# Where the steps of a recurrence and of an attention stand between the large matmuls of a projection: inverses begun earlier, attention two turns ahead, turns in pairs

## The chip, the core and the metric

The kernel runs on one core of a Trainium2 chip. The metric is the device time of one execution in microseconds (us), lower is better; the time before is the median of three runs. The engines are named as in the profile: PE is TensorE's matmul, PEld its weight load, DVE is VectorE, ACT is ScalarE, POOL is GpSimd, and SP is SyncE, which issues DMAs.

## What is computed

The reference is two programs in a row. The first (two layers of mixers, cross attention and a gated network of width 2816, 1024 columns, 512 rows) is not touched. The second is cut here to what matters:

```python
def second_block(x, c, norm_g, w_ada, b_ada, w_in, ...):
    h = rms_norm(x, norm_g) * (1.0 + scale) + shift
    proj = h @ w_in                                  # 512 x 1024 times 1024 x 4224
    ps, pa = token_shift(proj[..., :D_SHIFT], mu_shift), proj[..., D_SHIFT:]
    y_r, g_r = rwkv7_mix(ps, ...)                    # recurrence over 512 rows, 8 heads of 64
    q, ka, va, g_a = jnp.split(pa, 4, axis=-1)
    y_a = chunk_band_attention(q, ka, va, ...)       # 8 heads of 64, chunks of 64 rows
    y = jnp.concatenate([y_r * silu(g_r), y_a * silu(g_a)], axis=-1)
    return x + gate * (y @ w_out)                    # 512 x 1024 times 1024 x 1024

def rwkv7_step(state, inp):
    r_t, w_t, k_t, v_t, a_t, b_t = inp
    sa = einsum('bhij,bhj->bhi', state, a_t)
    state = state * w_t + sa * b_t + v_t * k_t
    return state, einsum('bhij,bhj->bhi', state, r_t)
```

## The kernel before

Every large product is taken in three passes (`mm3`, lines 365 to 367): operands are split into a high part XH or WH and a low part XL or WL, and three matmuls of 128x128 weights by 512 columns add up in one PSUM bank. I call these the large matmuls. ACT makes the high part of each chunk of weights (`hi_to`, L332), DVE the low part (`lo_to`, L342).

The second block is laid out in `dense_pe`, `dense_act`, `dense_dve` and `dense_pool`, one for each engine, in the same order. The projection has nine stages: k and w, and then seven, named in `BESIDE`, beside which the small work goes: r, v, aq, ak, g, av, ag. Each stage has 96 large matmuls. Between them `side()` is called: after every 12 large matmuls in r and v (8 calls each), after every 6 in the others (16 calls each). I number these calls 1 to 96 and call them places: r has 1 to 8, v 9 to 16, aq 17 to 32, ak 33 to 48, g 49 to 64, av 65 to 80, ag 81 to 96. At each place `side()` takes one turn (one `next`) of every generator that takes part in the stage. Each engine has its own copy of each generator; what one engine does in a turn and what another does in the same turn are tied by semaphores alone. All engines work their instructions off in this order, so that a wait holds all that is queued behind it.

The generators are:

- `rwkv`, the recurrence. Its turns in order: 10 of `prep`, 13 of the inverse of block 0 with `tail`, and then for t = 1, 2, 3 the 6 turns of `state(t-1)` beside the 12 of `inverse(t)` (`in_turns` takes one turn of each at a time and ends with the longest), with the 8 of `normed(t-2)`; at last `state(3)` beside `normed(2)`, and `normed(3)`. With one turn spent before place 1, `inverse(0)` stands at places 10 to 22, `inverse(1)` at 23 to 34, `inverse(2)` at 35 to 46, `inverse(3)` at 47 to 58, the state's turns at 23 to 28, 35 to 40, 47 to 52 and 59 to 64, and `normed(3)` at 67 to 74.
- An inverse (`inverse_pe`, L2530) takes a block of 128 rows through five levels. Its turn 0 makes the masked products "ba" (L2546) and its turn 1 the products "l" (L2561) and "ka" (L2546); from then on an even turn is "x" (L2575, 32 matmuls of 64x64) and an odd one "t" (L2589 and L2595, 32 each; in the last, turn 11, L2595 alone). Turn 4 adds four more products (L2609, L2616). DVE masks what comes out (L2656 to L2685), ACT copies (L2633, L2641). Turn 1 on DVE is the long one: L2668 to L2679 and two L2656.
- A state's three turns per chunk of 64 rows are "w" (L2712, added by DVE in four parts, L2764 and L2767, the last two of which empty the two banks), "u" (L2723) and "bd" with "by" (L2734, L2739).
- `norm_qk` at places 33 to 48 (behind four idle turns) and 49 to 60; its four transposes (L1889) fall on 44 to 47 and 56 to 59.
- `late`, the attention (`att_turns`, L1946): 38 turns and an end, behind four idle turns, so that its turn 1 is at place 69. An odd turn transposes the probabilities of two heads' row blocks (L1993, 2, 4, 6 or 8 transposes in all) and every fourth one first takes the product with the values (`values`, L2005); an even one makes scores (L1981) for two more, on which DVE adds the bias and takes the maximum (L2046 to L2051) and ACT the exponentials (L2017); DVE scales the probabilities of the turn before (L2060).
- `closing`, beside ag, makes the gate's row (L2878) and joins the recurrence's parts.

`key_sums_pe` (L2296) makes the sums of squares of the keys in four groups of four matmuls; the first group is taken ahead of stage r, and the other three, one each, after 3, 6 and 9 large matmuls of r (`each` in `gemm_c`).

After place 96 a loop of 11 passes (`second_pe`, `second_act`, `second_dve`) takes the rest of the attention, one turn in each pass, and beside it on PE one `out_part_pe` (6 large matmuls, a row block t and a chunk c of the first half of the last product). `out_part_pe(t, 0)` waits for `split_dve(t)`, which waits for `split_act(t)`; chunk 2 waits for the low part of its weights. Then come four parts of chunk 3 and 96 large matmuls of the second half, and DVE closes with the gate and the sum.

PSUM has 8 banks. `Banks.take` hands out the bank that has been idle longest in the order of the program, and the taker waits until the last reader of its former content has emptied it (`vacant`). While aq, ak or av runs, four banks are held by the stage, and four go round among all small work; each of the stage's is given back in its last four places (45 to 48 for ak).

## Time and profile before

| | us |
|---|---|
| median of three runs | 1762.18 (1760.67 to 1764.33) |
| the profiled execution, its own time | 1760.65 |
| its span, first to last instruction | 1758.8 |
| PE busy in it | 1728.8 |
| DVE busy | 1110.8 |
| ACT busy | 684.7 |
| POOL busy | 184.4 |

TensorE's granted clock is full (tenths 9) in all 40 slices of the page. The span is 1.85 us shorter than the execution's own time. A matmul is shown longer than it holds the engine: a large one is shown with 0.39 or 0.40 us, and the next starts 0.23 us after it, so that the busy share of PE hides short waits. What counts is the distance between starts.

### The profile page before, as it was taken

What the parts mean: (1) busy time and instruction counts of PE and PEld (TensorE: products, weight loads), DVE (VectorE), ACT (ScalarE), POOL (GpSimd) and SP (SyncE); (2) the same over time, 40 slices, a digit from 0 to 9 for tenths busy, and PEclk for the clock granted to TensorE, in tenths of its full rate; (3) what the DMA queues carried; (4) which work ended last, traced back from release to release, by engine and by line L of the source; (5) the groups of instructions that cost most, each with busy time, mean ns of one, the idle gap of its engine ahead of it and who ended that gap; (6) DMA issues with size and microseconds to landing.
All of it is one profiled execution on the core that took longest, in us unless ns stands there. A gap on an engine that the chain in (4) does not pass through costs nothing.

```text
span 1758.8 us, 27808 instructions
## 1 busy us (share of the span) xinstructions
PE 1728.8 (98%) x11461; PEld 1447.6 (82%) x11461; DVE 1110.8 (63%) x1624; ACT 684.7 (39%) x1045; POOL 184.4 (10%) x246
## 2 busy tenths in 40 slices
PE   8999999999999999999999999999998999999998
PEld 7888988988888879888998888888886767777766
DVE  5567266454568795454726755567988585566784
ACT  5332352232235643213235232223554543345452
POOL 4202001200011112000210200001112000011000
PEclk9999999999999999999999999999999999999999
DMA  9882912973345858833492265455683422112412
GB/s 301 259 217 99 252 39 79 279 230 110 126 138 186 260 166 204 247 97 118 114 283 77 83 204 156 143 183 185 201 277 108 153 65 81 34 43 62 169 37 84
DMA packets 175453, 270.44 MB, mean 154 GB/s; under 512 B 10488, under 2 KB 97780, under 8 KB 174560
## 3 DMA queue, kind: packets, MB, share of 16 engines
q1 hardware_dynamic: 147488, 189.90, 34.2%
q0 software_dynamic: 26368, 73.51, 15.7%
q10 hardware_dynamic: 1472, 5.26, 0.8%
q8 instruction: 91, 1.49, 0.4%
q14 instruction: 34, 0.28, 0.0%
HBM read 253.67 MB, written 61.09 MB: 179 GB/s over the span
## 4 chain that ended last, share of the span: by engine, by line
PE 88%; DVE 7%; issue 2%; ACT 1%; DMA 1%; POOL 1%; SPq 0%; ACTq 0%; DVEq 0%
PE ps L365 26%; PE ps L367 26%; PE ps L366 26%; DVE WL L342 2%; PE ps L1007 2%; PE ps L554 1%; PE ps L2575 1%; PE ps L2595 1%; PE ps L2589 1%; DMA RAW<-ffn_w_down 1%; PE ps L1981 0%; DVE SM L1637 0%; PE ps L2609 0%; DVE LATE L2656 0%; PE ps L2712 0%
## 5 line engine op out<-in xcount | busy, mean ns | idle before, releaser
L342 DVE TENSOR_TENSOR WL<-RAW,WH 128x1024 fp32r<-128x1024 f32 x325 | 393.3, 1222 | 387.7 <-ACT WH L332 387.2
L332 ACT ACTIVATE WH<-RAW 128x1024 fp32r<-128x1024 f32 x325 | 341.0, 1058 | 559.8 <-PE ps L367 450.6
L365 PE MATMUL ps<-XH,WH 128*128 128x512 f32 (+1 forms) x1416 | 524.6, 370 | 2.6 <-DVE WL L342 1.5
L367 PE MATMUL ps<-XH,WL 128*128 128x512 f32 (+1 forms) x1416 | 518.1, 366 | 0.0
L366 PE MATMUL ps<-XL,WH 128*128 128x512 f32 (+1 forms) x1416 | 517.9, 366 | 0.0
L365 PEld LDWEIGHTS ps<-XH,WH 128*128 128x128 f32 x1416 | 267.4, 189 | 50.1 <-issue 5.3
L367 PEld LDWEIGHTS ps<-XH,WL 128*128 128x128 f32 x1416 | 267.3, 189 | 43.3
L366 PEld LDWEIGHTS ps<-XL,WH 128*128 128x128 f32 x1416 | 267.5, 189 | 40.7
L365 PE MATMUL ps<-WH,XH 128*128 128x512 f32 x696 | 279.1, 401 | 7.9 <-DVE WL L342 7.0
L367 PE MATMUL ps<-WH,XL 128*128 128x512 f32 x696 | 271.9, 391 | 0.0
L366 PE MATMUL ps<-WL,XH 128*128 128x512 f32 x696 | 271.6, 390 | 0.0
L365 PEld LDWEIGHTS ps<-WH,XH 128*128 128x128 f32 x696 | 130.8, 188 | 39.5 <-DVE WL L342 8.0
L367 PEld LDWEIGHTS ps<-WH,XL 128*128 128x128 f32 x696 | 130.7, 188 | 27.8
L366 PEld LDWEIGHTS ps<-WL,XH 128*128 128x128 f32 x696 | 130.9, 188 | 25.4 <-issue 0.7
L721 POOL TENSOR_SCALAR SM<-SM 128x1 f32<-128x1 f32 x28 | 33.0, 1179 | 513.9 <-DVE SM L707 513.7
L1292 ACT ACTIVATE SCR<-SCR,VEC 128x512 f32<-128x512 f32 x44 | 31.8, 723 | 103.9 <-DVE SCR L1338 103.9
L561 ACT ACTIVATE XH<-ps 128x512 fp32r<-128x512 f32 x48 | 25.8, 599 | 98.6 <-PE ps L554 98.6
L1344 DVE TENSOR_TENSOR BIG<-SCR,ps 128x512 f32<-128x512 f32 x44 | 30.1, 688 | 31.6 <-ACT SCR L1292 31.6
L2633 ACT ACTIVATE SCR<-ps 128x512 f32<-128x512 f32 x32 | 17.4, 595 | 58.0 <-PE ps L2595 58.0
L365 PE MATMUL ps<-WH,MH 128*128 128x256 f32 (+1 forms) x136 | 39.5, 291 | 0.0
L366 PE MATMUL ps<-WL,MH 128*128 128x256 f32 (+1 forms) x136 | 39.4, 290 | 0.0
L367 PE MATMUL ps<-WH,ML 128*128 128x256 f32 (+1 forms) x136 | 39.4, 290 | 0.0
(404 smaller groups left out, 2063.7 us busy)
## 6 DMA issues: line engine op xcount, KB each, us to landing
RAW<-ffn_w_up SPq DMA_DIRECT2D x176, 256.0 KB, 3.5
weight_sums<-ffn_w_down POOLq DMA_DIRECT2D x12, 1536.0 KB, 18.5
RAW<-w_in SPq DMA_DIRECT2D x33, 512.0 KB, 3.9
RAW<-xa_wkv SPq DMA_DIRECT2D x32, 512.0 KB, 7.5
RAW<-weight_sums SPq DMA_DIRECT2D x32, 512.0 KB, 4.6
weight_sums<-ffn_w_down POOLq DMA_DIRECT2D x12, 1280.0 KB, 31.1
RAW<-c_w_in SPq DMA_DIRECT2D x24, 512.0 KB, 7.2
LATE<-w_ada SPq DMA_DIRECT2D x24, 512.0 KB, 5.2
```

The costliest lines, as they stand in the source:

```text
L332: e.activation(halves_of(i)[0][:, :, 0:w], raw(i)[:, :, 0:w], ACT.Copy).then_inc(*w_hi.up(i))
L342: e.tensor_tensor(wl[:, :, 0:w], raw(i)[:, :, 0:w], wh[:, :, 0:w].bitcast(F), ALU.subtract).then_inc(*w_lo.up(i))
L365: e.matmul(o, lh, rh, start=start, stop=False)
L366: e.matmul(o, lh, rl, start=False, stop=False)
L367: return e.matmul(o, ll, rh, start=False, stop=stop)
L554: r = e.transpose(b[:, 128 * k:128 * k + 128], x[:, 128 * (4 * q + k):128 * (4 * q + k) + 128], ident)
L561: e.activation(hi[:, 4 * q:4 * q + 4, 128 * t:128 * t + 128], k4(ps.tile((n, t, q))[:, :]), ACT.Copy).then_inc(*x_hi.up((n, t, q)))
L721: e.tensor_scalar(vr[:, t:t + 1], mv[:, t, 1:2], 1e-5, None, ALU.add).then_inc(*ln_g.up((n, t, "eps")))
L1007: r = e.matmul(b[:, 256 * (t % 2):256 * (t % 2) + 256], qT[:, 2 * h + k, 128 * t:128 * t + 128], KT[:, 2 * h + k, :], start=k == 0, stop=k ...
L1292: e.activation(gc[i], gc[i], ACT.Gelu_apprx_tanh, bias=vec(f"fcb{l}", j)).then_inc(*ffn_a.up(("gelu", l, j)))
L1344: e.tensor_tensor(hT[:, j, :], gc[i], ps.tile((("up", l, nb), i))[:, :], ALU.mult).then_inc(*ps.empties((("up", l, nb), i), ffn_v, ("h", l ...
L2575: r = e.matmul(bs[g][rows_of_x(lv, of[i], cp), 64 * i:64 * i + 64], BAs[t % 2][pps[cp], of[i], 0, :], Tt[pps[cp], in_t.index(of[i]), :], s ...
```

## The change

- The recurrence. The four inverses are made once and taken in parts. `inverse(1)` gives 10 of its 12 turns beside `state(0)`; its last two stand beside the first two of `inverse(2)`. The next 8 of `inverse(2)` stand beside `state(1)` and `normed(0)`, and its last two beside the first two of `inverse(3)`. The other 10 of `inverse(3)` stand beside `state(2)` and `normed(1)`. The rest is as it was.
- The attention begins behind two idle turns instead of four.
- In av and ag (`PAIRED`) nothing is done at an odd call of `side()`, and two turns of every generator at an even one.
- The loop after ag: PE takes two turns and two `out_part_pe` in each of four passes, and one last turn between the parts of chunk 2. ACT and DVE have 9 passes instead of 11, with the high and low parts of the weights moved.
- `key_sums_pe` is one piece ahead of stage r, and `each` is gone.

The diff, without the lines that only rename `four_behind(x)` to `behind(4, x)` for `norm_qk`:

```diff
-    def gemm_c(e, stage, nm, side=None, per=2, each=iter(())):
+    def gemm_c(e, stage, nm, side=None, per=2):
...
-                next(each, None)
...
+    PAIRED = ("av", "ag")
...
+        held = [0]
+
         def side():
-            for r in runs:
-                next(r, None)
+            held[0] += 1
+            turns = 1 if name not in PAIRED else 2 if held[0] % 2 == 0 else 0
+            for n in range(turns):
+                for r in runs:
+                    next(r, None)
...
-        sums = key_sums_pe(e)
-        next(sums)
+        key_sums_pe(e)
         next(run)
...
-            if t == 3:
-                r.then_inc(*pr_pe.up("kk8"))
-                ps.back("kk8")
-            yield
+        r.then_inc(*pr_pe.up("kk8"))
+        ps.back("kk8")
...
+        iv = [inverse(e, t) for t in range(4)]
         yield from prep(e)
-        yield from in_turns(inverse(e, 0), tail(e))
-        yield from in_turns(state(e, 0), inverse(e, 1))
-        yield from in_turns(state(e, 1), inverse(e, 2), normed(e, 0))
-        yield from in_turns(state(e, 2), inverse(e, 3), normed(e, 1))
+        yield from in_turns(iv[0], tail(e))
+        yield from in_turns(state(e, 0), turns_from(iv[1], 10))
+        yield from in_turns(iv[1], turns_from(iv[2], 2))
+        yield from in_turns(state(e, 1), turns_from(iv[2], 8), normed(e, 0))
+        yield from in_turns(iv[2], turns_from(iv[3], 2))
+        yield from in_turns(state(e, 2), iv[3], normed(e, 1))
         yield from in_turns(state(e, 3), normed(e, 2))
         yield from normed(e, 3)
 
-    def four_behind(run):
-        for n in range(4):
+    def turns_from(run, n):
+        for _ in range(n):
+            next(run)
+            yield
+
+    def behind(turns, run):
+        for n in range(turns):
             yield
         yield from run
...
-        late = four_behind(att_pe_run(e))
+        late = behind(2, att_pe_run(e))
...
-        for n in range(11):
+        for t in range(4):
             next(late, None)
-            if n < 8:
-                out_part_pe(e, n // 2, n % 2)
-            elif n < 10:
-                out_part_pe(e, n - 8, 2)
-        for t in (2, 3):
+            next(late, None)
+            for c in range(2):
+                out_part_pe(e, t, c)
+        for t in range(4):
+            if t == 2:
+                next(late, None)
             out_part_pe(e, t, 2)
...
     def second_act(e):
-        for n in range(11):
+        for n in range(9):
...
-            if n == 7:
+            if n == 5:
                 hi_to(e, n_out2 + 4)
...
     def second_dve(e):
-        for n in range(11):
+        for n in range(9):
...
-            if n == 8:
+            if n == 6:
                 lo_to(e, n_out2 + 4)
```

## Rows read from the trace of the kernel before

**Rows 1.** The page, part 1: busy time of each engine.

```profile
PE 1728.8 (98%) x11461; PEld 1447.6 (82%) x11461; DVE 1110.8 (63%) x1624; ACT 684.7 (39%) x1045; POOL 184.4 (10%) x246
```

**Rows 2.** Windows: stage ak, stage ag, attention's rest; columns PE, PEld, DVE, ACT, POOL.

```profile
1519.00:1573.00 54.00, 51.85 (x1080) 41.23 (x1072) 30.98 (x63) 22.83 (x44) 5.91 (x6) 1.00 0.15 42
...
1656.00:1697.00 41.00, 40.76 (x248) 29.66 (x246) 33.74 (x82) 21.16 (x58) 0.00 (x0) 1.00 0.17 51
1697.00:1725.00 28.00, 25.31 (x140) 17.40 (x139) 18.70 (x38) 14.09 (x34) 0.00 (x0) 1.00 0.18 57
```

**Rows 3.** Timeline of PE, places 29 and 30: start, length, line, operation.

```profile
1510.81 0.40 PE L367 MATMUL ps<-WH,XL 128*128 128x512 f32 x1
1511.14 0.69 PE L2575 MATMUL ps<-SCR,LATE 64*64 64x64 f32 x32
1511.76 0.50 PE L365 MATMUL ps<-WH,XH 128*128 128x512 f32 x1
1512.10 0.40 PE L366 MATMUL ps<-WL,XH 128*128 128x512 f32 x1
...
1513.03 0.39 PE L367 MATMUL ps<-WH,XL 128*128 128x512 f32 x1
...
1513.86 0.65 PE L2595 MATMUL ps<-SCR 64*64 64x64 f32 x32
1514.44 0.50 PE L365 MATMUL ps<-WH,XH 128*128 128x512 f32 x1
```

**Rows 4.** Timeline of PE at one group of the key sums.

```profile
1397.53 0.39 PE L367 MATMUL ps<-XH,WL 128*128 128x512 f32 x1
1397.76 0.95 PE L2296 MATMUL ps<-GB,LATE 128*128 128x8 f32 x8
1398.56 0.48 PE L365 MATMUL ps<-XH,WH 128*128 128x512 f32 x1
```

**Rows 5.** Timeline of PE at a turn of eight transposes, place 81.

```profile
1656.71 0.40 PE L367 MATMUL ps<-XH,WL 128*128 128x512 f32 x1
1656.95 1.03 PE L1993 MATMUL ps<-CST,GB 128*128 128x128 f32 x8
1657.74 0.48 PE L365 MATMUL ps<-XH,WH 128*128 128x512 f32 x1
```

**Rows 6.** Waits of PE from place 33 to the end: total, times, longest.

```profile
PE ps L2546 <- issue: 1.4, 2, 1.0
PE ps L365 <- DVE WL L342: 1.1, 1, 1.1
PE ps L365 <- issue: 0.9, 1, 0.9
PE ps L2589 <- DVE SCR L2685: 0.9, 2, 0.5
PE ps L1993 <- DVE GB L2060: 0.8, 2, 0.4
PE ps L2712 <- DVE GB L2775: 0.7, 1, 0.7
```

**Rows 7.** Timeline of DVE at places 35 and 36, where `inverse(2)` begins.

```profile
1527.34 0.77 DVE L2767 TENSOR_TENSOR LAST<-LAST,ps 64x256 f32<-64x256 f32 x2
...
1530.66 0.69 DVE L2668 TENSOR_TENSOR LATE<-LATE,GB 128x512 f32<-128x512 f32 x1
...
1533.88 1.28 DVE L2656 TENSOR_TENSOR LATE<-ps,GB 128x512 f32<-128x512 f32 x2
1535.08 1.22 DVE L342 TENSOR_TENSOR WL<-RAW,WH 128x1024 fp32r<-128x1024 f32 x1
```

**Rows 8.** Groups of DVE and ACT by line, 1697 to 1725: busy and mean ns.

```profile
L2051 DVE TENSOR_REDUCE SM<-GB 128x2 f32<-128x768 f32 (+1 forms) x2 | 2.2, 1086 | 0.1
L2928 DVE TENSOR_TENSOR XL<-LATE,XH 128x512 fp32r<-128x512 f32 x2 | 1.4, 692 | 1.6 <-ACT XH L2924 1.6
...
L2017 ACT ACTIVATE GB<-GB,SM 128x384 f32<-128x384 f32 (+1 forms) x4 | 2.6, 661 | 6.7 <-DVE SM L2051 6.7
```

More of the change, by code:

```diff
@@ L2140, in dense_pe @@
             else:
-                gemm_c(e, ("in2", name), 4, side, PER.get(name, 4), sums)
+                gemm_c(e, ("in2", name), 4, side, PER.get(name, 4))
     def silu_act(e, m):
@@ L2974, in second_pe @@
     def second_pe(e):
-        late = four_behind(att_pe_run(e))
-        dense_pe(e, rwkv(e, prep_pe, tail_pe, inverse_pe, state_pe, normed_pe), {"ak": four_behind(norm_qk_pe(e, 0)), "g": norm_qk_pe(e, 1)}, late, closing_pe(e))
-        for n in range(11):
+        late = behind(2, att_pe_run(e))
+        dense_pe(e, rwkv(e, prep_pe, tail_pe, inverse_pe, state_pe, normed_pe), {"ak": behind(4, norm_qk_pe(e, 0)), "g": norm_qk_pe(e, 1)}, late, closing_pe(e))
+        for t in range(4):
             next(late, None)
-            if n < 8:
-                out_part_pe(e, n // 2, n % 2)
-            elif n < 10:
-                out_part_pe(e, n - 8, 2)
-        for t in (2, 3):
+            next(late, None)
[4 more added lines that the diff above has]
+                next(late, None)
             out_part_pe(e, t, 2)
@@ L2989, in second_act @@
     def second_act(e):
-        late = four_behind(att_act_run(e))
-        dense_act(e, rwkv(e, prep_act, tail_act, inverse_act, state_act, normed_act), {"ak": four_behind(norm_qk_act(e, 0)), "g": norm_qk_act(e, 1)}, late, closing_act(e))
-        for n in range(11):
+        late = behind(2, att_act_run(e))
+        dense_act(e, rwkv(e, prep_act, tail_act, inverse_act, state_act, normed_act), {"ak": behind(4, norm_qk_act(e, 0)), "g": norm_qk_act(e, 1)}, late, closing_act(e))
+        for n in range(9):
             next(late, None)
@@ L3009, in second_dve @@
     def second_dve(e):
-        late = four_behind(att_dve_run(e))
-        dense_dve(e, rwkv(e, prep_dve, tail_dve, inverse_dve, state_dve, normed_dve), {"ak": four_behind(norm_qk_dve(e, 0)), "g": norm_qk_dve(e, 1)}, late, closing_dve(e))
-        for n in range(11):
+        late = behind(2, att_dve_run(e))
+        dense_dve(e, rwkv(e, prep_dve, tail_dve, inverse_dve, state_dve, normed_dve), {"ak": behind(4, norm_qk_dve(e, 0)), "g": norm_qk_dve(e, 1)}, late, closing_dve(e))
+        for n in range(9):
             next(late, None)
@@ L3033, in second_pool @@
         mask_pool(e)
-        dense_pool(e, rwkv(e, prep_own, tail_own, inverse_turns, state_turns, normed_pool), {"ak": four_behind(norm_qk_pool(e, 0)), "g": norm_qk_pool(e, 1)}, iter(()), iter(()))
+        dense_pool(e, rwkv(e, prep_own, tail_own, inverse_turns, state_turns, normed_pool), {"ak": behind(4, norm_qk_pool(e, 0)), "g": norm_qk_pool(e, 1)}, iter(()), iter(()))
     def out_part_pe(e, t, c):
```

## The prediction

> **What bounds the kernel now.** I read the busy times first [rows 1], then the windows by stage [rows 2], then the timeline of PE about single groups of small matmuls [rows 3 to 5], then PE's waits [rows 6], and last the queues of DVE and ACT where these waits arise [rows 7, 8]. PE is busy nearly all the time; DVE has 33.74 of 41 us in ag and 30.98 of 54 in ak, so it isn't full, and can only hold PE for short times where a turn needs it at once. The Trainium skill (Perfetto Trace Analysis, Identifying the Most-Contended Engine) warns that a matmul's busy share doesn't tell how near the peak PE is, and would go by the weight loads: here 82% against 98% [rows 1], so there is room inside a busy PE. The rows show the same: a large matmul is shown with 0.40 us though the next can start 0.23 us after it. So I count in distances between starts. The change removes no matmul. What it can save is what PE loses between kinds of work, and what it waits.
>
> **The price of a break.** At place 29, from the last large matmul before the group to the first after it are 1511.76 - 1510.81 = 0.95 us, less 0.23 for the large one itself: 0.72 for 32 small ones. At place 30 with 64 (L2589's 32 stand ahead of L2595's) it is 1.41 - 0.23 = 1.18 [rows 3]. So 32 more cost 0.46, and 0.72 - 0.46 = 0.26 is there whatever the number. The second large matmul after the group comes 0.34 after the first instead of 0.23, 0.11 more. A break for 64x64 work costs 0.37 us. Eight transposes take 1.03 - 0.23 = 0.80, which at 0.10 each leaves no fixed part [rows 5]; I give their break under 0.1. A group of key sums takes 0.80 as well, for eight records shown with 0.95 [rows 4]: again next to nothing but the loads.
>
> The Trainium skill (TensorEngine Tiling, Key Properties) says that going from one tiling mode to another drains TensorE. The rows agree: 64*64 pays 0.37, while 128*128 transposes, in the mode of the large matmuls, pay nearly nothing. It speaks against the pairs in av and ag: a pair of transposes and scores (64*128) still has both changes of mode, so nothing of that kind is saved.
>
> **Part by part.**
>
> *Key sums in one piece.* Three groups move ahead of stage r and lose their own break: 3 x 0.07 = 0.2 us (0 to 0.4). The wait for the squares stood ahead of the first group before too, and `lora` at place 1 is reached after the same work. The sums come 2 us earlier at DVE, but DVE's next step waits for `lora`, so that gives nothing.
>
> *Inverses begun earlier.* Places 10 to 64 all have 64x64 work now; after it 10 to 60. Four groups join others: 4 x 0.37 = 1.5 us. `normed(3)` ends at place 70 and not 74, beside nothing that waits for it. On SP's queue the loads that wait for the last "by" (`back_y`, `back_x`) can start four places sooner, before stage av's end, and no other DMA stands in another order.
>
> *Waits in ak and g.* These waits stand in rows 6 with 1.4, 0.9 and 0.7 (two more of 0.4 each are not shown): about 3.8 us in sum, most of it at places 36 to 38 and 48 to 50, right behind the first two turns of an inverse. That is where the change acts, for turn 1 is the long one on DVE: from L2668 to the end of the second L2656 4.5 us, and where `lo_to` comes behind it 1.2 more [rows 7]. After the change this turn stands at places 34 and 44, in one group with the last turn of the inverse ahead. There, with four banks in turn, "t" takes two, "l" two, and "ka" has to take those of "t" again: PE waits for ACT's two copies, about 0.5 us, as "ka" waited for the copies of "u" before (0.5 and 1.0).
> At place 34 the rest is lighter than it was at 36: no adds of the state stand ahead of it in DVE's queue, and `lo_to` comes two places later, at 36. I get 0.6 us for "x" at place 35, so 1.1 against 1.8 by the distances between starts.
> At place 44 it is heavier. `lo_to` stands at 44 itself, `norm_qk` holds one of the four banks from 44 on, and at 45 only three are free when the state's "w" takes two and "x" two: the second of "x" is that of the first "w". It is emptied by the third of DVE's four adds [two of them in rows 7, 0.77], behind 4.5 + 1.2. Counted from the start of PE's group at 44: DVE begins at 1.0, is through with "ka" at 5.7, with `lo_to` at 6.9, with the add at 8.1; PE has finished "w" at 6.0. So 2.1 us, with 0.4 for the bank of "w" and 0.5 for "ka" 3.0 us, against 2.5 now. Together 4.1 for 4.3: I take a gain of 0.2, between a loss of 3 (both queues one `lo_to` and the adds longer) and a gain of 2.
>
> *Attention in pairs.* Some 13 groups of transposes join the scores behind them, at 0.04 each 0.5 us (0 to 1.2). Between scores and their transposes stood 5 x 6 = 30 large matmuls, now 3 x 12 = 36, and between the scaling on DVE and the transposes 24 instead of 18, so DVE and ACT have more time, not less. The waits of DVE for PE come in fewer and longer pieces; it has 7 us to spare in the 41 of ag [rows 2].
>
> *The end of the attention.* From 1697 to 1725 PE has 28.00 - 25.31 = 2.7 us idle [rows 2], in four waits: 0.9 for the first split ahead of `out_part_pe(0, 0)`, 0.8 in two for scaled probabilities, 1.1 for the low part of chunk 2 [rows 6]. Each hides 0.17 more, for the matmul ahead of it is shown 0.17 longer than it holds the engine: 3.5 us. After the change two groups more (values and scores, over 4 us) stand ahead of `out_part_pe(0, 0)`, which covers the split; the waits for probabilities get 12 large matmuls (2.8 us) a step instead of 6; chunk 2 is wanted after 48 large matmuls behind the last scores, not after 30. Those three go. Two come. The values of the third pair stand two turns behind the copies of their last transposes with no large matmul between: 0.4 us. And on ACT `split_act(2)` now stands behind the last exponentials, which wait for DVE's maximum [rows 8]: my queue, from the last matmul of ag, is scores at 2.1, their maximum 4.4, two exponentials 5.7, tanh 6.2, three DVE operations of 0.69 8.2, the last scores (four operations of 0.42 to 0.48) and maximum 11.0, exponentials 12.4, the split on ACT 13.0 and on DVE 13.7. PE wants it at 12.7: 1.0 us. So 3.5 - 1.4 = 2.1 (from 0, where DVE arrives 2 us later, to 3.5).
>
> **The sum.** 0.2 + 1.5 + 0.2 + 0.5 + 2.1 = 4.5 us. Against the profiled execution: 1760.65 (span 1758.8 and 1.85 around it) becomes 1756.15. The median of the runs shown is 1.5 above that execution, so 1757.7.
>
> **Rivals.**
> 1. *The waits at the joined turns take it back.* For it: the three free banks at 45 and the queue of DVE. Against it: before 44 DVE has idle time. With the loss of 3 instead of the gain of 0.2 the sum is 1.3: 1761.
> 2. *Slower.* Both meetings of two inverses make PE wait for the whole of DVE's queue, 4.5 + 1.2 + 1.5 = 7.2 us each, as it would if "ka" and "x" got their banks only after DVE is empty. That is 14.4 for 4.3, less the 4.3 of the other parts: 5.8 slower, 1768. It decides from 8 us lost over the sum, 4 per meeting. Against it: PE's own work between covers 4 us of each queue, and at 34 no `lo_to` is in it.
> 3. *Every joined group saves a full break.* If the break weren't tied to the kind of matmul, the 13 pairs would give 13 x 0.37 = 4.8 instead of 0.5: 1753.4. Rows 5 speak against it. By the rule of the Trainium skill on drains (TensorEngine Tiling, Key Properties) it would not happen.
> 4. *The end is covered wholly* (DVE meets the last split in time) and the meeting at 34 costs nothing: 1.4 + 1.1 more, 1755.2.
> 5. *It doesn't do what it says:* DVE or ACT holds the new order back so that the four places saved turn up as waits of the state's chain ("w", "u", "bd") in g. Then only the end's 2 us are left: 1760. I count it with the first.
>
> **How the numbers follow.** Forecast 0.58, with its own range 1755.5 to 1760; rivals 1 and 5 0.22; rival 2 0.07; rival 3 0.04; rival 4 0.09. A measurement of this kernel tells 0.2% from no change, 3.5 us, which is 1758.7. Over two thirds of the forecast's range and rivals 3 and 4 lie below it: faster 0.55; rivals 1 and 5 and the rest: same 0.38; slower 0.07. The range takes in rival 4, nearly all of rival 3 and rival 1 with the runs' own spread of 2 us: 1753 to 1763.
>
> **What would show it.** Right: PE has no wait over 0.3 from place 62 to 96; the place at which "x" follows "w" (L2575 after L2712) with a wait of about 2 us once, for DVE L2767; `out_part_pe(0, 0)` without a wait; a wait of about 1 us for XL (L2919) in the third pass; from the first L2546 of the recurrence to its last "by" four places of six large matmuls less. A pair in ag should take as long as its two places, less 0.1. Wrong: waits over 3 us at the joined turns, or an ACT or DVE queue that puts the splits later than 15 us after ag.

## The result and the profile after

The changed kernel takes 1768.87 us (median of 8 runs, 1763.98 to 1771.27), the kernel before 1762.66 beside it; the ratio is 1.0031, 95% interval 1.0022 to 1.0041. It is slower, by about 6 us or 0.3%, and lies outside the range that was forecast. With all later runs of the kernel before, its median is 1762.2, against which the experiments are read.

The profiled execution has a span of 1767.3 us. Part 1 of its page answers to [rows 1]: DVE, ACT and POOL work within 2 us of what they did, PE is shown 5.0 us longer, with the same number of matmuls.

```profile
PE 1733.8 (98%) x11461; PEld 1453.4 (82%) x11461; DVE 1111.9 (63%) x1624; ACT 685.5 (39%) x1045; POOL 186.4 (11%) x246
```

More PE time for the same matmuls is a matter of the clock, or of matmuls that are stretched. So I laid the large matmuls of the two traces side by side: their order is the same in both, and the time from the start of one to the start of a later one tells where time went. The times in the first column are those of the kernel before.

| Stretch of the kernel before | before | after | difference |
|---|---|---|---|
| 10.7 to 1329.6, untouched | 1318.88 | 1318.96 | +0.1 |
| 1329.6 to 1388.0, untouched | 58.40 | 60.89 | +2.5 |
| 1388.0 to 1427.9, key sums | 39.84 | 43.07 | +3.2 |
| 1427.9 to 1468.6, before the states | 40.79 | 40.76 | 0.0 |
| 1468.6 to 1727.5, recurrence and attention | 258.84 | 261.71 | +2.9 |
| 1727.5 to 1754.5, last output chunks | 26.97 | 26.97 | 0.0 |

The first stretch, which no kernel here changes, takes between 1318.8 and 1325.6 us in the profiles of the kernels below. So where single profiles are compared, it is stretch by stretch and not by their totals.

**The key sums.** The program's 16 narrow matmuls stand in the profile as 32 records of 8 columns; they are counted as records here. The windows of PE of the changed kernel (columns: window, length, PE busy, granted clock, DMA share, GB/s) show a granted clock of 0.50, that is its 1.2 GHz level, from within the group of sums on (half from 1401.2, for 6.8 us):

```profile
1398.00:1402.50 4.50, 4.50 (x35) 0.86 0.40 117
1402.50:1407.50 5.00, 5.00 (x14) 0.50 0.01 3
1407.50:1412.00 4.50, 4.50 (x18) 0.94 0.00 0
```

In the profile of the kernel before no window of this stretch is under 1.00; two of them, with the five engines' busy times ahead of the clock:

```profile
1398.00:1402.00 4.00, 4.00 (x30) 3.75 (x30) 0.09 (x1) 1.85 (x2) 0.00 (x0) 1.00 0.42 123
1402.00:1406.00 4.00, 4.00 (x18) 2.12 (x17) 0.64 (x3) 2.43 (x4) 0.00 (x0) 1.00 0.00 0
```

The timeline of PE (start, length, line, operation) has the group itself, the counterpart of [rows 4], and the large matmuls behind it, whose starts are 0.43 us apart and not 0.23:

```profile
1398.58 4.42 PE L2300 MATMUL ps<-GB,LATE 128*128 128x8 f32 x32
1402.85 0.77 PE L365 MATMUL ps<-XH,WH 128*128 128x512 f32 x1
1403.42 0.63 PE L366 MATMUL ps<-XL,WH 128*128 128x512 f32 x1
1403.85 0.63 PE L367 MATMUL ps<-XH,WL 128*128 128x512 f32 x1
```

PE waits for nothing here and is shown busy 4.50 of 4.50 us; when the clock fell it had done matmuls of 8 columns and nothing else for 2.6 us, since 1398.58. The Trainium skill (TensorE: Matmul & The Clock Gate, Part 1: The HAM clock gate) ties this clock to how busy the engine has been, and gives 0.427 us from start to start for 512 columns at the low level. The rows agree with that distance (0.43), and they show that work can be dense in the timeline and the clock fall all the same.

The 2.5 us of the untouched stretch are a fall too (granted clock 0.5 from 1346.6 to 1353.4). A second profile of the changed kernel (f3 below) has none there, and those of a1, a2, a3, b1 and others have one. So it comes and goes between executions of one program; whether the change makes it more frequent is not shown.

**The recurrence and the attention.** PE's waits from place 33 to the end (total, times, longest) answer to [rows 6]. The changed kernel's lines stand a few lower or higher: its L2548, L2577, L2591, L2597 and L2687 are L2546, L2575, L2589, L2595 and L2685 of before. In the same way the first values are L2004 or L2005, the gates L2880 or L2884, the diagonals L2901 or L2905, the keys' squares L1904 or L1905 and their sums L1915 or L1916.

```profile
PE ps L2577 <- issue: 3.5, 2, 1.8
PE ps L2597 <- DVE SCR L2687: 1.7, 1, 1.7
PE ps L2004 <- ACT VL L2197: 1.3, 1, 1.3
PE ps L2880 <- DVE SCR L2901: 1.2, 1, 1.2
PE ps L365 <- DVE XL L2921: 0.8, 1, 0.8
PE ps L2548 <- ACT LATE L2635: 0.8, 2, 0.4
```

Of [rows 6] the wait for L342, that for the first split and those for L2060 are gone, as forecast. In their place stand four that were not in the sum: 1.75 of the first row (place 43), L2597 (place 54), L2004 (the turn of place 81, now taken at 82) and L2880 (83, now at 84). The rest of the first row is place 45, 1.73, which was forecast with 2.1.

### The profile page after: what moved, and what is told of

Read it like the earlier page. It is cut to its first block, busy times and chain, and to the rows that moved or that the text cites. A ratio compares the mean times of both kernels' runs of the same rounds, so it can differ in the third digit from the quotient of the medians.

```text
span 1767.3 us, 27808 instructions
## 1 busy us (share of the span) xinstructions
PE 1733.8 (98%) x11461; PEld 1453.4 (82%) x11461; DVE 1111.9 (63%) x1624; ACT 685.5 (39%) x1045; POOL 186.4 (11%) x246
## 3 DMA queue, kind: packets, MB, share of 16 engines
q8 instruction: 91, 1.49, 0.3%
## 4 chain that ended last, share of the span: by engine, by line
PE 89%; DVE 7%; issue 2%; DMA 1%; ACT 1%; POOL 1%; SPq 0%; ACTq 0%; DVEq 0%
PE ps L365 26%; PE ps L367 26%; PE ps L366 26%; DVE WL L342 2%; PE ps L1006 2%; PE ps L553 1%; PE ps L2577 1%; PE ps L2597 1%; DMA RAW<-ffn_w_down 1%; PE ps L2591 1%; PE ps L2004 1%; PE ps L1980 0%; PE ps L2611 0%; PE ps L2736 0%; DVE SM L1636 0%
## 5 line engine op out<-in xcount | busy, mean ns | idle before, releaser
L342 DVE TENSOR_TENSOR WL<-RAW,WH 128x1024 fp32r<-128x1024 f32 x325 | 393.4, 1222 | 389.8 <-ACT WH L332 389.4
L715 DVE SCALAR_TENSOR_TENSOR XR<-XR,SM,GB 128x1024 f32<-128x1024 f32 x24 | 30.8, 1283 | 12.5 <-POOL SM L722 12.5
```

Of the source, the lines that this page charges most:

```text
L342: e.tensor_tensor(wl[:, :, 0:w], raw(i)[:, :, 0:w], wh[:, :, 0:w].bitcast(F), ALU.subtract).then_inc(*w_lo.up(i))
L715: e.scalar_tensor_tensor(out=x, in0=x, scalar=rs[:, t:t + 1], in1=b, op0=ALU.mult, op1=ALU.add).then_inc(*ln_v.up((n, t)))
```

## The experiments

Each kernel is built from the kernel before or from the changed one. The diffs are shortened; a comment says what isn't shown. "+3.8" means against the 1762.2 of the kernel before; "clock" is the mean granted clock of all runs of a kernel. That of the kernel before is 0.9992, that of the changed kernel 0.9965; 0.001 of a span is 1.8 us. A run's clock is given to 0.001, and it varies from run to run, so that the mean of a kernel is uncertain by 0.0001 to 0.0003, that of a2 by 0.0005 and that of the changed kernel by 0.0006.

**Each part alone.** Four kernels before with one part of the change each.

```diff
 a1  -        sums = key_sums_pe(e)
     -        next(sums)
     +        key_sums_pe(e)             # all four groups at once, none in stage r
 a2  +        yield from in_turns(iv[1], turns_from(iv[2], 2))   # the new rwkv, nothing else
     +        yield from in_turns(iv[2], turns_from(iv[3], 2))
 a3  +    PAIRED = ("av", "ag")          # the new side(), nothing else
 a4  +        late = behind(2, att_pe_run(e))   # with the new loops of the end, no pairs
```

> The kernel before with one edit: the key sums in one piece ahead of stage r. Theory C (the clock): behind 16 small matmuls in a row the granted clock of TensorE falls to half for some 5 us, as in the profile of the changed kernel (0.50 from 1402.5 to 1407.5, large matmuls at 0.43 us a step), so this edit alone costs 3 us, in the profile and in the median, with the same fall in its trace. Theory Q (only the queues behind the joined turns cost): no change, -0.2 us as forecast, and the fall in the changed kernel's profile was chance, as the one at 1350 us in work that both kernels share (2.4 us).

> The kernel before with one edit: the new order of the inverses. Theory Q: the waits at places 43 to 45 and 54 (1.7 us each in the changed kernel) come back here, and the edit costs 2 to 4 us net of the 1.5 that four breaks less give. Rival (these waits come from the other edits, which make DVE and ACT late): -1.5 us.

> The kernel before with one edit: two turns at every second place in av and ag, the attention still behind four turns and the end as before. Theory D (pairs save no break and make waits): the wait of the gate's row for its diagonals (1.2 us) and that for the first values (1.3 us) appear, so +1 to +3 us. Forecast of the prediction: -0.5. Rival B (every joined group saves a full break): -4.

> The changed kernel with the key sums, the order of the inverses and the single turns of before: what is left is the attention two turns earlier and the new loop after ag. Theory: -2.1 us as forecast for the end, as the changed kernel's profile has it (25.4 us from the last matmul of ag to the end of the last values, 28.6 before, less 0.85 of work moved ahead). Rival (the earlier attention meets the rows of av that ACT has not copied yet, 1.3 us at the first values): -0.8.

| Kernel | us | ratio to before | clock |
|---|---|---|---|
| a1, sums in one piece | 1766.02 (+3.8) | 1.0026 [1.0017, 1.0035] | 0.9972 |
| a2, recurrence | 1764.67 (+2.5) | 1.0018 [1.0007, 1.0028] | 0.9979 |
| a3, pairs | 1761.12 (-1.1) | 0.9995 [0.9986, 1.0004] | 0.9995 |
| a4, early attention and the end | 1766.61 (+4.4) | 1.0034 [1.0022, 1.0045] | 0.9989 |

a1 cost somewhat more than its theory C said (3), and a2 came inside its 2 to 4. For a3 theory D failed: the pairs brought no wait and no cost, and the forecast of -0.5 lies in the interval. For a4 both values failed: it lost 4.4 where a gain of 2.1 or 0.8 was expected.

Three of four parts cost something alone, and the sum of all, 9.6, is more than the 6.2 to 6.7 that they cost together. So two parts help each other; it turns out to be a3 and a4.

**The sums: one part undone, half and twice the dose.**

```diff
 u1  # the changed kernel with gemm_c(..., each) and key_sums_pe as before: four groups of eight
 c1  # the kernel before, two groups of sixteen
     -            yield
     +            if t % 2:
     +                yield
 e1  # the kernel before, one piece, done twice over
     -        for t in range(4):
     +        for t in (0, 1, 2, 3, 0, 1, 2, 3):
```

> The changed kernel with one part undone: the key sums stand again as four groups of eight in stage r (each followed by two large products), everything else stays as changed. Theory C (the clock): 32 narrow matmuls in a row let the granted clock fall in many executions, and that is all that the single edit costs; undoing it gives back what it cost alone, 3.8 us: about 1765.0 against 1768.9 of the changed kernel, ratio to before 1.0012 to 1.0022, and the mean granted clock of its runs is nearer to 0.999 than to 0.996. Rival L (layout): the change of the time comes from where instructions fall in memory and not from the sums; then nothing comes back, 1768 to 1769. Places 43, 45 and 54 should show the same waits as in the changed kernel (1.8, 1.7, 1.7 us) if they belong to the recurrence.

> The kernel before with the key sums in two groups of sixteen (the first ahead of stage r, the second after its first large product of three matmuls) in place of four groups of eight. Half the dose. Theory C (clock falls that a long dense group of narrow matmuls brings): a group of sixteen takes 1.6 us in place of 3.2, so falls are rare; 1762.2 to 1763.5, runs at a clock of 0.999 or more. Rival O (order: it costs because the first large matmuls of r wait for something that the earlier sums hold up, or because PE is simply that much longer): the cost follows the share that is moved, half of 3.8: 1764.

> The kernel before with the key sums in one piece and done twice over (64 narrow matmuls in a row; the second 32 write the same numbers again). Twice the dose. The added work itself is 32 more at 0.1 us: 3.2 over the 1766.0 of the one piece, 1769.2. Theory C (clock falls come with the length of the dense narrow group): a fall in nearly each execution, longer than before, mean clock of the runs under 0.997: 1770 to 1773, and the profile shows the clock at half behind the group. Rival O (the one piece costs by its place or order, clock or no clock): 1769 and a clock as of the one piece, 0.997.

u1: 1764.71 (ratio 1.0016 [1.0007, 1.0025], clock 0.9988), 4.2 less than the changed kernel. c1: 1763.86 (1.0011 [1.0002, 1.0019], clock 0.9983). e1: 1770.63 (1.0051 [1.0038, 1.0064], clock 0.9962). The profile of e1 has the fall again, with the clock at 0.52 in the second half of its 64 narrow matmuls and behind them; windows of all engines, the clock ahead of the DMA share:

```profile
1399.00:1404.50 5.50, 5.50 (x50) 5.43 (x48) 1.17 (x2) 2.60 (x3) 0.00 (x0) 1.00 0.34 98
1404.50:1411.50 7.00, 7.00 (x27) 6.23 (x27) 0.54 (x2) 0.23 (x1) 0.00 (x0) 0.52 0.00 0
```

In eights, sixteens and thirty-twos the same work is done in the same bank; the clock goes 0.9992, 0.9983, 0.9972, and the time follows: 1.4, 3.0 and 4.9 us of the span are what these clocks leave out, 1.6 and 3.5 more than before, measured +1.7 and +3.8. For e1 the clock gives 5.3 more, with the 3.2 us of added work 8.5, measured +8.4. The clock explains nearly all of the cost, in the mean of the runs. The profiles say the same from the other side: the stretch of the key sums takes 39.84 us before, 39.83 in c1 and 39.82 in a1, whose profiles have no fall there, but 43.07 and 43.01 in the two of the changed kernel, which have one. So the new order of the sums costs nothing while the clock holds, and it doesn't give the forecast 0.2 either.

That of a1 (clock 1.00 from 1396 to 1412) has two falls elsewhere, at 921.7 and 1355.2, in work that no edit touches. So a single profile is a weak witness of how often the clock falls, and where the falls of the runs without a profile stood is not shown. c1 lies between what its two theories gave; falls are rarer there, not absent. Why the clock falls with narrow matmuls is not settled by this.

**The recurrence: which wait is what.** At place 45 of a2 the timeline of PE has "w", the wait, "x" at half speed, and the first large matmul at half speed behind it:

```profile
1569.70 1.11 PE L2712 MATMUL ps<-GB,XR 64*128 64x64 f32 x16 [0.18 <-DVE LATE L2656]
1572.54 1.14 PE L2575 MATMUL ps<-SCR,LATE 64*64 64x64 f32 x32 [1.73 <-issue]
...
1574.37 0.78 PE L365 MATMUL ps<-WH,XH 128*128 128x512 f32 x1
```

and DVE's queue in the same time has `lo_to` (L342) ahead of the adds that empty the banks of "w":

```profile
1568.92 1.28 DVE L2656 TENSOR_TENSOR LATE<-ps,GB 128x512 f32<-128x512 f32 x2
1570.12 1.21 DVE L342 TENSOR_TENSOR WL<-RAW,WH 128x1024 fp32r<-128x1024 f32 x1
1571.25 0.74 DVE L2764 TENSOR_TENSOR BIG<-BIG,ps 64x256 f32<-64x256 f32 x2
1572.02 0.76 DVE L2767 TENSOR_TENSOR BIG<-BIG,ps 64x256 f32<-64x256 f32 x2
```

Two kernels take away what makes it wait: c2 moves the low parts in ak from the last place of four to the first; d1 also moves the normalisation of the queries (places 37 to 48) to 33 to 44, so that its transposes leave the bank before place 45, and that of the keys one place later.

```diff
 c2  -                    if n == (3 if name == "ak" else per // 2) and (name, c) != ("r", 3):
     +                    if n == (0 if name == "ak" else per // 2) and (name, c) != ("r", 3):
 d1  -        {"ak": four_behind(norm_qk_pe(e, 0)), "g": norm_qk_pe(e, 1)}     # c2, and so on
     +        {"ak": behind(0, norm_qk_pe(e, 0)), "g": behind(1, norm_qk_pe(e, 1))}   # each engine
```

> The kernel before with the recurrence's new order alone (1764.67 measured), and in stage ak DVE makes the low parts of the next weights behind the first turn of four, not behind the last: at places 33, 37, 41, 45 in place of 36, 40, 44, 48. Theory Q (DVE's queue holds the bank of the state's w): at place 45 the wait of L2577's counterpart for the bank, 1.73 us, falls to 0.3 to 0.6, and with it the clock fall right behind it (1 us) goes; 1762.2 to 1763. Theory F (at place 43 PE runs out of instructions because the fetch of the next 16 KB comes late while a weight load keeps the DMA engines at 0.9 busy): the load is released by these low parts and starts about 3 places earlier, so the stop of 1.2 us at place 43 becomes smaller or stands elsewhere: 1 us more, 1761.5. Rival B (banks: two of four are free whatever DVE does): the 1.73 stay, 1764.5. Rival S (the stop at place 43 belongs to the instructions there, not to the load): it stays at place 43.

> The recurrence's new order with the early low parts (1763.08 measured), and two shifts more: the normalisation of the queries starts at place 33 and not 37, so its transposes stand at 40 to 43 and its bank is back before place 45; that of the keys starts at 50 and not 49, so its last square no longer stands in ACT's queue behind the four operations of the normed rows. Theory N (both waits are what they look like: at 45 a bank that the transposes hold, at 54 DVE's reduction standing in front of L2685's counterpart and waiting for ACT): the 1.37 at place 45 falls under 0.4, the 1.69 at place 54 goes, and what the four fewer breaks save shows: 1760.2 to 1761. Rival W (waits move: the transposes at 40 to 43 hold a bank where the inverse wants one, or DVE's earlier reductions stop the joined turns at 34): as much is lost again, 1763.

c2: 1763.08 (1.0005 [0.9996, 1.0014], clock 0.9989), 1.6 less than a2. In the profiles the stretch of recurrence and attention falls from 261.15 us in a2 to 258.84, what it takes in the kernel before. The wait at 45 is 1.37, not the 0.3 to 0.6 expected of the queue alone: with `lo_to` out of the way DVE itself waits 0.68 for the last of "w", and then the banks come free by its third add:

```profile
1567.66 0.74 DVE L2764 TENSOR_TENSOR BIG<-BIG,ps 64x256 f32<-64x256 f32 x2 [0.68 <-PE ps L2712]
1568.44 0.76 DVE L2767 TENSOR_TENSOR BIG<-BIG,ps 64x256 f32<-64x256 f32 x2
```

So most of the wait is a round trip over a bank that was just written. A fall of the clock for 3.4 us, begun in this wait or up to 0.4 us behind it, is in the profiles of a2, u1 and both of the changed kernel (wait 1.73), and not in c2 (1.37) or d1. The second profile of a2 (f4) has the wait of 1.73 and no fall; without it and with 0.29 more of the stop at place 43 its stretch takes 0.52 us less, so the fall costs about 0.8 us.

In the mean of all runs the clock may have a larger share in a2: 0.9979 leaves out 2.3 us more than the 0.9992 of the kernel before, with an uncertainty of 0.9, and +2.5 is measured. But without the fall the stretch of its profiles still takes 1.5 to 1.8 us more than before, which is waits. The two are more than was measured, so how the cost is shared between waits and clock stays open.

d1 settles the bank: "x" follows "w" with no wait worth the name,

```profile
1573.02 1.11 PE L2712 MATMUL ps<-GB,XR 64*128 64x64 f32 x16 [0.19 <-DVE LATE L2656]
1574.28 0.69 PE L2575 MATMUL ps<-SCR,LATE 64*64 64x64 f32 x32
```

but the time is 1763.94 (1.0013 [1.0005, 1.0022]), 0.9 more than c2. That alone is hardly clear of the noise; the stretch in the profiles, neither of which has a fall there, says the same, 260.72 us against 258.84. The rival was right, the waits moved. The longest of PE's waits of d1 from place 33 to 64:

```profile
PE ps L2595 <- DVE SCR L2685: 1.5, 1, 1.5
PE ps L2546 <- issue: 1.1, 2, 0.6
PE ps L2723 <- DVE LAST L2767: 1.0, 1, 1.0
PE ps L2575 <- DVE LATE L2656: 0.8, 1, 0.8
```

Its first row is place 54, where my mending failed. In the changed kernel DVE stood idle there for the keys' last square (L1904), with L2687, for which PE waits, behind it; and ACT had done the four operations of the normed rows (L2820) first:

```profile
1607.29 0.69 DVE L1915 TENSOR_REDUCE SM<-LAST 128x8 f32<-128x512 f32 x1 [3.59 <-ACT LAST L1904]
...
1608.10 0.74 DVE L2103 SCALAR_TENSOR_TENSOR SCR<-ps,VEC,SCR 128x511 f32<-128x511 f32 x1
1608.76 0.75 DVE L2687 TENSOR_TENSOR SCR<-ps,GB 128x256 f32<-128x256 f32 x2
```

```profile
1604.25 1.09 ACT L2635 ACTIVATE SCR<-ps 128x512 f32<-128x512 f32 x2 [3.14 <-PE ps L2597]
1605.22 1.51 ACT L2820 ACTIVATE LAST<-ps,VEC 128x128 f32<-128x128 f32 x4
1606.59 0.66 ACT L1904 ACTIVATE LAST<-VL 128x512 f32<-128x512 f32 x1
```

A shift by one place only put the third square there instead of the fourth. f1 is c2 with the keys four places later, f2 is f1 with the pairs and with PE's last turns in twos.

```diff
 f1  -        "g": norm_qk_pe(e, 1)}
     +        "g": four_behind(norm_qk_pe(e, 1))}           # each engine
```

> The recurrence's new order with the early low parts (1763.08 measured), the queries' normalisation back at place 37, and that of the keys started four places later, at 53, so that all its squares stand behind the normed rows of place 52 in ACT's queue. In the kernel before this one it was moved by one place, which only put its third square behind them in place of its fourth, and 1.48 stayed. Theory N: the 1.69 at place 54 goes, nothing else of the recurrence moves (1.37 at place 45 stays): 1761.3 to 1761.8. Rival W (the keys' transposes, now at 60 to 63, or the squares beside the last state's turns stop PE there): no gain, 1763 or more.

f1: 1763.08 (1.0005 [0.9996, 1.0014]), nothing gained on c2. The wait at 54 falls from 1.69 to 0.96; the rest is L2103, which waits for ACT's L2096, again behind the normed rows. And 0.3 more comes at place 58 and 0.5 at 61. The turn with the four ACT operations moved from place 54 to 52; in the old place PE waited for nothing behind it. I take that for the cause, and the squares only for the first to be held up. It is read from the queues: no kernel was run with `normed(1)` alone back at its old place.

**Place 43: PE without instructions.** In the changed kernel PE stops in the middle of a group, 19 of 32 matmuls done, for 1.75 us and for no semaphore:

```profile
1563.02 0.56 PE L2577 MATMUL ps<-SCR,LATE 64*64 64x64 f32 x19
1565.33 0.39 PE L2577 MATMUL ps<-SCR,LATE 64*64 64x64 f32 x11 [1.75 <-issue]
```

The profile shows q8 as a queue of instructions. It brings 91 packets of 16 KB, against 22922 matmuls and weight loads, 252 for a packet; I take them for PE's. The records of PE and PEld from one packet to the next are 130 to 400, mostly 200 to 300. DMA queues of the changed kernel, first 1554.50 to 1562.70, where q8 has no packet and a load of weights keeps the engines at 0.9 at the end, then 1562.70 to 1564.00:

```profile
DMA  0000000000000000000000001000004243699999
...
q1 hardware_dynamic: 896, 0.46, 19.2%
q14 instruction: 1, 0.01, 0.4%
```

```profile
q8 instruction: 1, 0.02, 5.0%
```

465 records lie between this fetch and the one before it. Two kernels were profiled a second time to see whether this varies between executions of one program.

> The changed kernel once more, for a second profile. If the clock's fall behind the key sums belongs to the kernel, it stands again at 1401 to 1405; if the stop at place 43 depends on when a fetch of instructions meets the weight load, it has another length than 1.75 us; the waits at 34, 45, 54, 81 and 83 are set by the order of the queues and come out within 0.05 of 0.38, 1.73, 1.70, 1.30 and 1.23.

> The recurrence's order alone once more, for a second profile. Theory F (fetch against load): the stop at place 43 (1.20 before) changes with the time of the fetch: between 0 and 1.8, and small where the fetch comes before the load fills the DMA engines. Rival S: 1.20 again. The wait at 45 and, if it belongs to that wait, the clock's fall behind it stand again.

| Profile | records to this fetch | stop inside the group |
|---|---|---|
| changed, first | 465 | 1.75 |
| changed, again | 467 | 1.49 |
| a2, first | 435 | 1.20 |
| a2, again (f4) | 467 | 1.49 |
| u1 (same recurrence) | 314 | none |
| c2 (low parts early) | 343 | none |
| kernel before | 302 | none |

Where the fetch comes ahead of the load (u1, c2) there is no stop; in the four with a stop it lands at the load's end, and PE stops at the same matmul of the program each time. In the kernel before it comes 0.5 us behind the load's last packet, after 302 records, and PE doesn't stop. In all four PE goes on 1.3 to 1.6 us behind the end of the fetch, whenever that is (it ends at 1563.79 in the first row and 1559.31 in f4), so the stop is shown to end with it. u1 and a2 run the same instructions there, so it isn't the instructions alone. In c2 the load starts together with place 43's group, in a2 2.4 us ahead of it: not earlier, as I had expected, but later against PE's work, and that was enough. That speaks for theory F.

It has two weak points. Nothing here shows the time at which a fetch is asked for, so that the load delays it is inferred. And in u1 the load also starts 2.4 us ahead of place 43; its fetch came 1.9 us before the load, after 314 records, where in the four with a stop 330 to 365 records had passed when the load began and no fetch had come. Why it came earlier in u1 isn't shown. f3 also had the clock's fall at the sums again (half from 1399.5, for 6.8 us) and the waits of 45, 54, 81 and 83 within 0.02 of the first profile (1.73, 1.70, 1.31, 1.21); it took 1766.90 and f4 1763.62.

**The attention.**

```diff
 b1  # the changed kernel with the sums and the recurrence of before:
     # left are the attention two turns ahead, the pairs and the new end
```

> The changed kernel with its key sums and its recurrence undone: what is left are the attention two turns ahead, the pairs, and the new end. Theory A (early attention costs because at place 81 the values wait for the last rows of av on ACT and at 83 the gates wait for the diagonals on DVE; pairs soften both): in the profile 1.3 at place 81 and 1.2 at place 83 as in the changed kernel, and about 1.7 less at the end than before: 1762 to 1763, that is 1 to 2 us above the pairs with the mended end (1760.8). Rival (early attention costs only alone, with pairs it gives its gain): 1760. Rival (it costs as much in pairs): 1765.

b1: 1762.69 (1.0004 [0.9996, 1.0013]), theory A as expected. (Its profile ran 1764.30; it has a fall of the clock, 3.4 us from 1647.1, 1.6 us behind the wait in the first row.) PE's waits from 1640 on:

```profile
PE ps L1981 <- issue: 1.7, 1, 1.7
PE ps L2005 <- ACT VL L2199: 1.3, 1, 1.3
PE ps L2884 <- DVE SCR L2905: 1.2, 1, 1.2
PE ps L365 <- DVE XL L2925: 0.8, 1, 0.8
```

against those of a4, without pairs (its gates also met a fall of the clock, 3.4 us from 1671.2):

```profile
PE ps L2005 <- ACT VL L2199: 2.7, 1, 2.7
PE ps L2884 <- DVE SCR L2905: 2.6, 1, 2.6
PE ps L365 <- DVE XL L2925: 1.4, 1, 1.4
```

Two turns earlier the first values need the rows of v before ACT has moved the last of them (`row_act` at place 80), and the gates need diagonals that stand in DVE's queue behind scaled scores. Pairs put six large matmuls more ahead of each, so the waits halve: that is why a3 and a4 cost less together than apart. The first row of b1 (place 74, where `normed(3)` ends; a4 has it with 0.78) isn't in the changed kernel, whose recurrence, four places shorter, is over by then. That it is a wait for a bank wasn't tested by itself.

**Better than both?** c3 is the kernel before with the pairs, and PE's turns in twos at the end; d2 is d1 with the same.

```diff
 c3  -        for n in range(11):
     -            next(late, None)                # one turn ahead of each out_part_pe
     +        for t in range(4):
     +            next(late, None)
     +            next(late, None)                # two ahead of each row, three more in pass 3
```

> The kernel before with the pairs in av and ag (1761.12 alone) and, in PE's order alone, the last turns of the attention in twos ahead of each row of the first two passes of the output product, with the last three turns ahead of the third pass's first three groups. Recurrence, key sums and the start of the attention as before; ACT and DVE keep their order, the split of the first row included. Theory E (what the end of the changed kernel saves comes from the pairs ahead of the output product, and needs no earlier attention): the wait of 0.9 for the first split goes, the waits for scaled probabilities halve; the third pass may wait up to 1 us for the later splits; 1 to 2 us less than the pairs alone: 1759 to 1760.2. Rival D (DVE's order sets the end; PE's new order only moves the waits): 1761 as the pairs alone.

> That kernel together with the pairs in av and ag and PE's order at the end (1760.8 for these two without the recurrence). If the parts add up as their separate times do: before - 1.4 - (0.8 to 2 from the recurrence) = 1759 to 1760. Rival (the parts disturb one another, as pairs and early attention do in the changed kernel): 1761 or more.

> That kernel with the pairs in av and ag and PE's order at the end (1760.8 for these two alone). The recurrence then has four fewer breaks and waits of some 2.6 us in ak and g where the kernel before has some 3.8 in other places; if both sums hold, 1759 to 1760, the fastest of all; if the recurrence gives nothing, 1760.8.

c3: 1760.80 (0.9990 [0.9981, 0.9998]), the fastest of all, 1.4 under the kernel before, though not told apart from a3. For the end its rival was right: PE's waits from 1690 are what they were in [rows 6] (the 0.8 for the probabilities not shown again), with the 0.9 for the split now 1.0 ahead of the values instead,

```profile
PE ps L365 <- DVE WL L342: 1.1, 1, 1.1
PE ps L2005 <- issue: 1.0, 1, 1.0
```

so its gain is that of the pairs (1761.12), and what the end of the changed kernel saves does come from the earlier attention. d2: 1763.02 (1.0003 [0.9993, 1.0012]); f2: 1762.58 (1.0005 [0.9996, 1.0014]), above both values given for it. Both are slower than c3: with the waits mended as far as I could, the recurrence's new order still costs 1.8 to 2.2 us. For d2 none of this is the clock (0.9998, c3 0.9996), for f2 (0.9988) it may be 1.3 of the 1.8.

Side by side, the stretch from 1468.6 to 1727.5 of the kernel before in each profile:

| Kernel | us | Kernel | us |
|---|---|---|---|
| before | 258.84 | d1 | 260.72 |
| changed, both profiles | 261.71, 261.62 | f1 | 259.30 |
| a2, both profiles | 261.15, 260.63 | b1 | 261.26 |
| c2 | 258.84 | c3 | 257.75 |
| a3 | 257.74 | d2 | 260.47 |
| a4 | 264.38 | f2 | 258.98 |

## Why the prediction was wrong

From the kernel before by way of b1 and u1 to the changed one, the time goes 1762.2, 1762.7, 1764.7, 1768.9. The three steps are attention +0.5 (forecast -2.6), recurrence +2.0 (forecast -1.7) and key sums +4.2 (forecast -0.2): the miss of 11 us is 3.1, 3.7 and 4.4. Each step is the difference of two medians and uncertain by about 1 us. By the mean clocks, up to 4.8 of the 6.7 us that the changed kernel takes more are falls of the clock, which the forecast had nowhere.

**Key sums: a term was missing.** The step that failed is "A group of key sums takes 0.80 as well", "again next to nothing but the loads", and the term of 0.2 made from it. It was right for eight. With 32 in a row the granted clock falls, for 6.8 us in both profiles of the changed kernel, at 3.2 us each time. Nothing in the trace of before shows it, since there the longest such group is eight; but the range held no bound for it either ("0 to 0.4"), though the sum moved matmuls of another shape together.

**Recurrence: the breaks were right, the waits were not.** Four fewer breaks save about 1.3 us, forecast 1.5. From place 33 to 65 PE of c2 waits 5.7 us, and PE of the kernel before 4.4 (the 3.8 of the prediction and 0.6 for L2801). c2 waits 1.3 more, and yet both take 258.84 us over the stretch from 1468.6 to 1727.5. Of the waits at the joined turns, place 34 cost 0.39 for "ka" (forecast 0.5) and 0.13 for "x" (0.6); place 44 0.39 (0.5); place 45 1.73 + 0.17 (2.1 + 0.4). That is 2.8 for 4.1, better than forecast. What failed is "I take a gain of 0.2": I priced the places where the inverses meet and no place behind them. Place 54 (1.70) came from a move that the text states ("`normed(3)` ends at place 70 and not 74, beside nothing that waits for it") but follows only for the last of the normed runs; `normed(1)` moved too, and stands beside the keys' squares. Place 43 (1.2 to 1.75) could not be read from the trace of before as a price; that a load and a fetch meet there could be seen, with 302 records to the fetch. The fall at place 45 (about 0.8 us where it comes) is a third term, at nothing in the sum.

**Attention: the end was right, its start was not.** The pairs gave 1.1 (a3) and, on f1, 0.5, forecast 0.5. The end went as worked out: from the last large matmul of ag to the first behind the last values 25.4 us, before 28.6; about 0.8 of the difference is scores that now stand ahead of it, so the end gave about 2.4, forecast 2.1. The first split has no wait, and the third pass waits 0.8 for XL (forecast 1.0). What failed is "DVE and ACT have more time, not less", and the test "PE has no wait over 0.3 from place 62 to 96": it was worked out for scores and transposes, whose partners moved along, and not for `row_act` and `closing_dve`, which stayed where they were while their users moved two turns ahead: 1.30 and 1.22.

**The rivals.** None had the mechanisms. Rival 2 gave the right size (1768) by luck: no joined turn waited for the whole of DVE's queue. Rival 5 came nearest in kind, four saved places that come back as waits, but at places that it didn't name.

## What to carry to other kernels

When runs of turns are shifted against each other, list for every one of them what stays behind: who produces for it, what stands at its new place on each engine, and which bank it holds; price the shifted partners (here 1.7 + 1.3 + 1.2 us), not only the place at which the change is aimed. Leave narrow matmuls spread among the large ones, even where their own break costs nothing. And where single edits of 1 to 4 us are in question, look at the mean clock over all runs beside the time: it told the sums' 3.8 us from a wait, where a1's own profile had no fall at the sums.

## What the runs showed of the hardware

- The granted clock fell to its 1.2 GHz level inside a row of 32 and of 64 matmuls of 8 columns with PE shown busy all the time (0.50 for 6.8 us), and the mean clock of the runs was 0.9992, 0.9983, 0.9972 and 0.9962 for rows of 8, 16, 32 and 64. One profile of 32 had no fall there.
- It also fell, for 3.4 us, in four of the five profiles with a wait of 1.73 us at place 45, and in none of the five of the new recurrence where that wait was 1.37 or less (c2, d1, d2, f1, f2). In b1 it fell 1.6 us behind a wait of 1.74. The length of a wait doesn't decide it alone: behind the waits of 1.70 at place 54 (1.69 in c2) no profile has a fall.
- PE stopped for 1.2 to 1.75 us in the middle of a group in four profiles where the next 16 KB packet of q8 came 435 to 467 records after the last, at the end of a 512 KB load, and went on 1.3 to 1.6 us behind its end. Up to 403 records no stop was seen.
